# One gather per pick for both expert tables, and weights made for two picks at a time

## The reference

```python
q = (xb @ w_query).reshape(tb, PEER_HEADS, 2, PEER_KEY_DIM // 2)
s = jnp.einsum('thpd,pnd->thpn', q, sub_keys)
top_s, top_i = lax.top_k(s, k)                                    # k = 16, of 2 x 128 keys
cand_s = top_s[:, :, 0, :, None] + top_s[:, :, 1, None, :]
best_s, best_j = lax.top_k(cand_s.reshape(tb, PEER_HEADS, k * k), k)
...
gate = jax.nn.softmax(best_s, axis=-1)
u = expert_u[idx]                                                 # tables of 16384 x 1024
act = jax.nn.gelu(jnp.einsum('thkd,td->thk', u, xb))
w = gate * act
return jnp.einsum('thk,thkd->td', w, expert_v[idx])
```

## Time and profile before

| | |
|---|---|
| median of 3 runs | 1893.31 us (1893.27 to 1904.49) |
| the profiled execution | 1906.0 us, of it the span 1904.2 us |
| busy in the span: PE, DVE, ACT, POOL | 1487.1, 1110.6, 357.7, 1052.6 us |
| moved | 616.74 MB, mean 324 GB/s |

### The profile page before, as it was taken

The page is one execution under the profiler, slowest core; times in us unless marked ns, Lnnn a source line. Parts: engine busy times, 40 slices in busy tenths (PEclk is TensorE's granted clock), DMA queues, the critical chain, the costliest instruction groups (busy, mean ns, idle before and its releaser), DMA issues.

```text
span 1904.2 us, 14545 instructions
## 1 busy us (share of the span) xinstructions
PE 1487.1 (78%) x4063; PEld 675.9 (35%) x4063; DVE 1110.6 (58%) x2719; ACT 357.7 (19%) x910; POOL 1052.6 (55%) x1111
## 2 busy tenths in 40 slices
PE   8999977498887774799988874988888738767776
PEld 3466544145322221344433522433334313222222
DVE  3344255686555555765786656666876556645552
ACT  1033202112221111121221111221211211111110
POOL 1111033666666666556676565766665657656664
PEclk9999997798999987899989997999999979998999
DMA  5112046999998888799999997999999889988897
GB/s 180 63 72 74 15 168 237 418 345 350 370 384 353 352 342 348 294 362 392 417 418 418 370 381 301 396 418 417 418 418 399 319 331 356 384 338 347 346 383 260
DMA packets 184126, 616.74 MB, mean 324 GB/s; under 512 B 19275, under 2 KB 20811, under 8 KB 184054
## 3 DMA queue, kind: packets, MB, share of 16 engines
q0 software_dynamic: 152064, 553.72, 74.5%
q1 hardware_dynamic: 31990, 62.17, 8.7%
HBM read 614.77 MB, written 1.05 MB: 323 GB/s over the span
## 4 chain that ended last, share of the span: by engine, by line
PE 30%; DVE 19%; DMA 15%; issue 14%; POOL 13%; another core or an unknown queue 8%; ACT 0%; DVEq 0%; SPq 0%; POOLq 0%
POOL arena L607 13%; PE bank L892 11%; DMA arena<-peer_u,idx 9%; PE bank L685 8%; DVE arena L1602 8%; DMA arena<-peer_v,idx 5%; PE bank L866 2%; PE bank L787 2%; PE bank L793 2%; DMA wring<-gla_w_in 1%; PE bank L748 1%; PE bank L759 1%; DVE best L1549 1%; PE bank L841 1%
## 5 line engine op out<-in xcount | busy, mean ns | idle before, releaser
L892 PE MATMUL bank<-arena 128*128 128x512 f32 x1920 | 953.7, 636 | 339.6 <-DMA arena<-peer_v,idx 164.5
L1602 DVE CUSTOM_DVE_ANT_0 arena<-arena,bank 128x1024 f32<-128x1024 f32 x528 | 625.3, 1217 | 274.2 <-DMA arena<-peer_u,idx 188.1
L607 POOL DMA_INDIRECT arena<-peer_u,idx x528 | 511.7, 969 | 337.9 <-issue 140.0
L892 PEld LDWEIGHTS bank<-arena 128*128 128x128 f32 x1920 | 359.9, 199 | 892.3 <-issue 454.6
L607 POOL DMA_INDIRECT arena<-peer_v,idx x528 | 511.2, 968 | 281.6 <-issue 149.7
L685 PE MATMUL bank<-wring,hT 128*128 128x512 f32 (+5 forms) x604 | 262.2, 589 | 5.0 <-issue 2.8
L1197 ACT ACTIVATE arena<-con,wgt 128x128 f32<-128x128 f32 x480 | 153.3, 390 | 356.3 <-issue 170.6
L685 PEld LDWEIGHTS bank<-wring,hT 128*128 128x128 f32 (+1 forms) x604 | 108.8, 182 | 151.7 <-issue 145.1
L1186 ACT ACTIVATE gl<-dots 128x16 f32<-128x16 f32 x33 | 7.1, 216 | 401.3 <-issue 228.8
L572 POOL TENSOR_TENSOR small<-small,con 128x1 f32<-128x1 f32 (+2 forms) x12 | 8.1, 677 | 120.3 <-DVEq L1368 71.1
L1611 DVE SCALAR_TENSOR_TENSOR h<-arena,wgt,h 128x1024 f32<-128x1024 f32 x48 | 61.6, 1284 | 20.7 <-DMA arena<-peer_v,idx 20.7
(11 more groups left out here) (157 smaller groups left out, 1011.3 us busy)
## 6 DMA issues: line engine op xcount, KB each, us to landing
wring<-gla_w_in SPq DMA_DIRECT2D x12, 2048.0 KB
arena<-peer_u,idx POOLq DMA_INDIRECT x528
arena<-peer_v,idx POOLq DMA_INDIRECT x528
wring<-gla_w_out SPq DMA_DIRECT2D x4, 2048.0 KB
wring<-peer_w_query SPq DMA_DIRECT2D x4, 2048.0 KB
wring<-attn_w_in SPq DMA_DIRECT2D x2, 2048.0 KB
wring<-attn_w_out SPq DMA_DIRECT2D x2, 2048.0 KB
gws<-peer_w_query SPq DMA_DIRECT2D x2, 2048.0 KB, 10.3
```

What stands on the lines that cost most here:

```text
L607: nc.gpsimd.indirect_dma_start(out=ring[:, slot, :], out_offset=None, in_=table.rearrange("l e d -> (l e) d"), in_offset=bass.IndirectOffs ...
L892: last = nc.tensor.matmul(yacc[:, 512 * i:512 * i + 512], wdiag[:, k, :], vrow[:, v_slot(g, k), 512 * i:512 * i + 512], start=first, stop= ...
L1602: v.tensor_tensor_reduce(out=rows, in0=rows, in1=xnow, scale=1.0, scalar=0.0, op0=ALU.mult, op1=ALU.add, accum_out=dots[:, g % 2, k:k + 1] ...
```

## The change

It lays the two tables side by side on the host, outside the measured time, as `peer_uv` with rows of 8 KB. One gather brings a pick's pair of rows into one ring of eight pairs, and a pair's slot is free when its v rows have been mixed or added. GpSimd issues one gather where it issued two. Gelu, weight and diagonal are made for pairs of picks: `gelus(i, j)` when both dots are done, `weigh` after the dot that follows them, `diagonals(i, j)` after that. TensorE mixes tile i in tile i, so `FIRST` moves each mixer pass a tile earlier, `add_experts` comes at pick 3 of the next tile, and 33 rounds stand where 34 stood. The selection is cut in three, after dots 1, 4 and 7, in every tile. Tile 0 has all of tile 1's selection after its dot 7. VectorE no longer takes six picks of the last tile. ScalarE's pieces have places by pairs (-1 is ahead of the first). In the windowed attention the products of block 2 with block 0, which its mask makes zero, are dropped, and a transpose of block 0 is narrower.

```diff
-U_RING, V_RING = 8, 9
+RING = 8
...
-LEAD = 4
-ADD_BEHIND = LEAD + 2
+GROUP = 2
+GROUPS = TOPK // GROUP
...
-        FIRST = {1: 10, 2: 18}
+        FIRST = {1: 9, 2: 17}
...
-        TENSOR_AT = ((7, 11, 12, 15), (1, 2, 5, 9), (2, 3, 8, 9, 12), (0, 4, 6, 10, 12), (2, 6, 10), (0, 3, 12), (0, 5, 9, 12))
+        TENSOR_AT = ((7, 11, 12, 15), (1, 2, 5, 9), (2, 3, 8, 9, 12), (0, 4, 6, 10, 12), (2, 4, 10), (0, 3, 12), (0, 5, 9, 12))
         VECTOR_AT = ((5, 10), (8, 12), (4, 14), (12,), (3, 6, 10), (10, 12), ())
-        SCALAR_AT = ((3,), (0, 2, 3), (0, 2), (0, 1, 2), (0, 1, 2), (0,), (0, 1), (0,))
+        SCALAR_AT = ((5,), (-1, 1, 4, 5), (-1, 3, 6), (2, 3), (-1, 0, 3), (-1,), (-1, 1, 4), (-1,))
...
-            if g == TILES - 1:
-                return LAST_SHARE
-            return SHARE if mixer_turn(g + 1)[0] and mixer_turn(g + 1)[1] < len(TENSOR_AT) else ()
+            return SHARE if mixer_turn(g)[0] and mixer_turn(g)[1] < len(TENSOR_AT) else ()
...
-            def gather(kind, g, k):
-                layer = GATHERED[g][0]
+            def gather(g, k):
                 n = TOPK * g + k
-                if kind == 0:
-                    at_least(pool, u_used, n - U_RING + 1)
-                elif n >= V_RING:
-                    wait_second_used(pool, (n - V_RING) // TOPK, (n - V_RING) % TOPK)
-                table, ring, landed = ((io["peer_u"], urow, u_in), (io["peer_v"], vrow, v_in))[kind]
-                slot = n % (U_RING, V_RING)[kind]
+                if n >= RING:
+                    wait_second_used(pool, (n - RING) // TOPK, (n - RING) % TOPK)
                 nc.gpsimd.indirect_dma_start(
-                    out=ring[:, slot, :], out_offset=None, in_=table.rearrange("l e d -> (l e) d"),
-                    in_offset=bass.IndirectOffsetOnAxis(ap=idx[:, g % 4, k:k + 1], axis=0)).then_inc(landed[slot], 16)
-            def chosen(g):
-                pool.wait_ge(idx_ready, g + 1)
+                    out=uvrow[:, n % RING, :], out_offset=None, in_=io["peer_uv"].rearrange("l e d -> (l e) d"),
+                    in_offset=bass.IndirectOffsetOnAxis(ap=idx[:, g % 4, k:k + 1], axis=0)).then_inc(uv_in[n % RING], 16)
...
-            chosen(0)
-            for k in range(U_RING):
-                gather(0, 0, k)
-            small_root(1)
-            for k in range(U_RING, TOPK):
-                gather(0, 0, k)
-            for k in range(8):
-                gather(1, 0, k)
-            chosen(1)
-            for k in range(TOPK):
-                gather(0, 1, k)
-                if k < 8:
-                    gather(1, 0, k + 8)
-            for i in range(2, TILES + 1):
+            for i in range(TILES):
                 full, turn = mixer_turn(i)
-                if i < TILES:
-                    chosen(i)
+                pool.wait_ge(idx_ready, i + 1)
                 for k in range(TOPK):
-                    if i < TILES:
-                        gather(0, i, k)
-                    if k >= LEAD:
-                        gather(1, i - 1, k - LEAD)
-                    elif i > 2:
-                        gather(1, i - 2, TOPK - LEAD + k)
-                    if k == 13 and i in (2, EARLY, 26):
+                    gather(i, k)
+                    if k == 5 and i == 0:
+                        small_root(1)
+                    if k == 10 and i in (2, EARLY, 26):
                         small_root({2: 2, EARLY: 0, 26: 1}[i])
-                    if k == 13 and full and turn == 0 or k == 15 and full and turn == 5:
+                    if k == 10 and full and turn == 0 or k == 14 and full and turn == 5:
                         small_root(full)
                     if k == 11 and full and turn == 4:
                         root(gms[:, 0:4], gms[:, 4:8], 4)
-            for k in range(TOPK - LEAD, TOPK):
-                gather(1, TILES - 1, k)
             small_root(2)
...
+            def head_values(hh, windowed):
...
                 for b in range(NB):
-                    for kb in range(b + 1):
+                    keys = range(1, 3) if windowed and b == 2 else range(b + 1)
+                    for kb in keys:
                         n = live_parts(kb)
                         at = KEY_BLOCKS.index((b, kb)) if kb else b
                         last = nc.tensor.matmul(bk(6, b * HD, b * HD + HD), probT[0:n, int(kb == 0), at * P:at * P + P],
-                                                v_all[0:n, kb, hh, :], start=(kb == 0), stop=(kb == b))
+                                                v_all[0:n, kb, hh, :], start=(kb == keys[0]), stop=(kb == b))
...
-                    wait_landed(pe, 1, g, k)
+                    wait_landed(pe, g, k)
                     pe.wait_ge(diag_ready, MIXED[g] + mine.index(k) + 1)
                     for i in range(2):
                         last = nc.tensor.matmul(yacc[:, 512 * i:512 * i + 512], wdiag[:, k, :],
-                                                vrow[:, v_slot(g, k), 512 * i:512 * i + 512], start=first, stop=last_one)
+                                                rows_of(g, k, 1)[:, 512 * i:512 * i + 512], start=first, stop=last_one)
...
-            for i in range(1, TILES + 1):
+            for i in range(TILES):
...
-                    mix(i - 1, (k,))
+                    mix(i, (k,))
...
-                    if k == 3 and i + 2 < TILES and not late:
+                    if k == scores_at and 0 < i and i + 2 < TILES:
                         scores(i + 2)
-                    if k == 4 and full and turn == 6:
-                        scores(i + 1)
-                    if k == 13 and full and turn == 6:
-                        scores(i + 2)
...
-            def gelus(g):
-                act.wait_ge(dots_ready, g + 1)
-                nc.scalar.activation(gl[:, :], dots[:, g % 2, :], ACT.Gelu_apprx_tanh).then_inc(gelu_ready, 1)
-            def diagonals(g, half):
-                act.wait_ge(wgt_ready, g + 1)
+            def gelus(g, j):
+                c = slice(GROUP * j, GROUP * j + GROUP)
+                act.wait_ge(u_used, TOPK * g + GROUP * j + GROUP)
+                nc.scalar.activation(gl[:, c], dots[:, g % 2, c], ACT.Gelu_apprx_tanh).then_inc(gelu_ready, 1)
+            def diagonals(g, j):
+                act.wait_ge(wgt_ready, GROUPS * g + j + 1)
                 for k in by_tensor(g):
-                    if k // (TOPK // 2) != half:
+                    if k // GROUP != j:
...
+                for j in range(GROUPS):
+                    gelus(i, j)
+                    if j == GROUPS - 1 and i + 1 < TILES and (i == 0 or GATHERED[i + 1][2] == 0):
+                        take_rows(i + 1)
+                    diagonals(i, j)
+                    if j in at:
+                        next(pieces)
+                    if j == 2 and i + 1 < TILES:
+                        gate_exps(i + 1)
+                    if j in (2, 4, 7) and i == 3:
+                        take_queries(0, 2, (2, 4, 7).index(j))
+                    if j == 6 and i == 2:
+                        take_T("tr_ffn0", 2)
+                        take_gains(2)
...
-            def choose_experts(g):
-                layer = GATHERED[g][0]
+            def choose_sums(g):
                 best16(cand[:, :], cand_rest[:, :], best, best_j)
...
                 dve.sem_inc(best_ready, 1)
+            def choose_experts(g):
...
-                wait_landed(dve, 0, g, k)
-                rows = urow[:, u_slot(g, k), :]
+                wait_landed(dve, g, k)
+                rows = rows_of(g, k, 0)
                 v.tensor_tensor_reduce(out=rows, in0=rows, in1=xnow, scale=1.0, scalar=0.0,
                                        op0=ALU.mult, op1=ALU.add, accum_out=dots[:, g % 2, k:k + 1]).then_inc(u_used, 1)
-                if g and k - ADD_BEHIND in by_vector(g - 1):
-                    add_second(g - 1, k - ADD_BEHIND)
...
-                wait_landed(dve, 1, g, k)
                 at_least(dve, v_added, ADDED[g] + by_vector(g).index(k))
-                v.scalar_tensor_tensor(out=h[:, b, :], in0=vrow[:, v_slot(g, k), :], scalar=wgt[:, g % 2, k:k + 1], in1=h[:, b, :],
+                v.scalar_tensor_tensor(out=h[:, b, :], in0=rows_of(g, k, 1), scalar=wgt[:, g % 2, k:k + 1], in1=h[:, b, :],
                                        op0=ALU.mult, op1=ALU.add).then_inc(v_added, 1)
-            def dotted(g):
-                dve.wait_ge(gate_exp, g + 1)
+            def weigh(g, j):
                 zs = z[:, g % 2, :]
-                steps.did(v.reciprocal(zs[:, 2:3], zs[:, 1:2]))
-                dve.wait_ge(u_used, TOPK * (g + 1))
-                dve.sem_inc(dots_ready, 1)
-            def weigh(g):
-                zs = z[:, g % 2, :]
-                if g >= 2:
-                    dve.wait_ge(diag_ready, MIXED[g - 1])
-                    at_least(dve, v_added, ADDED[g - 1])
-                steps.settle()
-                dve.wait_ge(gelu_ready, g + 1)
```

(50 more changed lines are left out.)

71 lines of the change are left out of this document (20 added, 51 removed).

## The result

| | kernel before | changed kernel |
|---|---|---|
| median, us (runs) | 1893.64 (4) | 1789.53 (4) |
| lowest to highest | 1893.27 to 1904.49 | 1780.09 to 1794.79 |
| profiled span | 1904.2 | 1789.1 |

A forecast was written before the change was run, and what follows sets the result against it. It took the DMA engines at 418 GB/s (2.51 us per pick) as the bound, with VectorE's gaps slowing clean tiles. Stage terms summed to 1805.5 us against the profiled 1904.2, scaled to 1795 us; range 1735 to 1890.

The forecast's parts named there:

- The main term: Clean tiles, which load no weights: a single gather removes nearly all of VectorE's gaps, 48 to 40.5 us each.
- the gaps: VectorE's idle time in the selection, 15.5 us in one clean tile; rival that they stay, chance 0.12, about 1885 us.
- A sign of being wrong that came: Clean tiles: the prediction is wrong if GpSimd waits more than 5 us at a time.
- its two others: Signs of being wrong: mixer passes below 370 GB/s, or VectorE's gaps of 4.71 us still there.
- The rival of eight pairs too few: Ring: tolerance passed three times a tile, +5 us in each of 26 tiles, median 1924 us; chance 0.13.
- the slot's turn of 14.8 us: Ring: time a pair holds its slot; eight pairs tolerate interruptions of 5.3 us in clean tiles, 8.9 in mixer tiles.
- Start: First tile: pick 4 of tile 1 done at 343 us instead of 331, 12 us lost to GpSimd's wait for slot 0.
- Second pass: Second mixer pass: seven mixer tiles at 50 us each, 350 us, the same value as the first pass.
- Gathers: GpSimd: one 1 MB gather costs between 0.95 and 1.9 us, taken as 0.95; 144 or 272 packets a pair.
- the rival "better": Gathers and mixer tiles: 8 KB rows move faster or mixer tiles reach 47.5 us, median 1736 us; chance 0.10.
- The rule on queues: Weight loads: DMA engines switch queues only between packets, so 8 KB packets could delay weights, TensorE standing 7 us each pass.
- the rival of late weights: Mixer passes: TensorE waits twice 7 us and some for lower clock, median 1815 us; chance 0.03.

The follow-up runs named there:

- experiment 1: Changed kernel with each pair brought by two 512 KB gathers again: 1926.96 us, ratio 1.017 to the kernel before.
- experiment 9: On one chip: the kernel before unchanged (1871.42 us profiled), the changed kernel (1785.64 us), and the changed kernel with two gathers per pair (1925.53 us).
- experiment 8: Changed kernel with start in original order, GpSimd clearing 128x800 and then 128x400 elements of an unread buffer behind each gather: 1804.28 us.
- experiment 10: Changed kernel with a second gather of 64 bytes a row into an unread buffer behind each gather: 1825.30 us.
- the other start: Changed kernel with tile 1's choice spread over the first eight products and two query groups moved after picks 3 and 9 of tile 0: 1788.42 us.
- experiment 3: Changed kernel with GpSimd clearing an unread 128x800 buffer behind each gather: 1808.46 us, ratio 0.954 to the kernel before.
- experiment 2: Kernel before with v gathers bringing 2 KB a row instead of 4: 1882.18 us, ratio 1.008 to the kernel before.
- experiment 6: Changed kernel with the other start, eight pairs: 1788.42 us, ratio 1.030 to the kernel before.
- experiment 7: Changed kernel with nine pairs and the other start together: 1738.23 us, ratio 1.002 to the kernel before.

## Why the prediction was right, and where it wasn't

*Stage by stage.* The terms of the sum against the changed kernel's trace (1789.1 us, of a run of 1790.87):

| stage | predicted us | measured us |
|---|---|---|
| start to tile 1 | 343 | 333.8 |
| tiles 1 to 5 | 231 | 229.9 |
| clean tiles 6 to 8 | 121.5 | 123.0 |
| seven mixer tiles | 350 | 349.8 |
| tile 16 | 41 | 46.2 |
| second pass | 350 | 340.2 |
| tiles 24, 25 | 82 | 82.4 |
| tiles 26 to 30 | 203 | 199.4 |
| end | 84 | 84.4 |
| together | 1805.5 | 1789.1 |

The sum was 16 us too high. It was then scaled by 0.994, since the profiled run of before was a long one, to 1795. The profiled run of the changed kernel was an ordinary one, so that 1795 lies within 6 us of the median is in part luck.

*The main term, clean tiles from 48 to 40.5.* The number is right: 39.9 to 41.0, and the sign it named is there: no idle time ahead of the second MAX8 (L1498), DMA share 1.01. That the gaps go with the single gather was a pattern read from 33 choices. Experiments 1 and 9 bear it out in part, on chips of the first kind: two gathers bring back waits behind the unknown releaser, though hardly in VectorE's choice. The mechanism was seen too narrowly. "Taken alone this is worth nothing while the DMA engines set 2.51" doesn't hold on this kind of chip: with hardly a gap in the choice, two gathers still make a clean tile 46.8 us, and in the second profile of the kernel before GpSimd waits only 2.7 us for VectorE in five clean tiles and yet they take 45.3 each. What the prediction says beside it, "GpSimd is exactly as slow as the DMA engines and never gets ahead", fits better: at 2.50 us a pick GpSimd can't make up for a wait, whatever it is for (table of experiment 9). By itself this pace is a small term, at most 16 us in experiment 8 and 37 in experiment 10, both on the second kind, where GpSimd has few waits on top.

*A sign of being wrong that came.* The prediction called itself wrong if GpSimd waits more than 5 us at a time in clean tiles. It does, seven times in nine clean tiles and 7.81 us at the longest, and costs nothing there: the DMA share stays at 1.01. The sign was set too sharply; its two others (mixer passes below 370 GB/s, gaps of 4.71 us) stayed away, at 389 and 391 GB/s.

*What wasn't seen: the gain belongs to a kind of chip.* The working took the gaps for a property of the kernel. That the comparison fell on a chip of the first kind is luck: on the second kind the time would have lain in the range, but the forecast "faster" would have been wrong. On two of the chips the kernel before takes 1735 us, 157 less, while forms of the changed kernel take what they take on the first kind: 1788.4 with the other start on the second kind, 1785.6 and 1789.5 for the changed one on the first. The changed kernel itself wasn't run on the second kind; from the form with the other start, whose tile 1 comes 5 us sooner, the change makes it some 3% slower there. No profile of the kernel before exists from such a chip, so that its stalls are absent there is inferred from its time and from the profiles of the others. What makes the stalls, and why on some chips, stays open. A full queue (the changed kernel has one, without stalls) and a GpSimd busy half of the time (experiment 3) are ruled out as sufficient, and a full queue isn't needed either (experiment 2). An unbroken row of gathers on a chip of the first kind, with rows of 8 KB, wasn't tested.

*The ring.* The rival of eight pairs too few was set at 3.3 us per tile; it didn't decide, but it is real. With the other start, nine pairs are 50 us faster than eight (1738.2 and 1788.4 on one chip); of that, 1.9 and 2.7 us are saved in each mixer tile of the two passes, 2.4 in each of tiles 1 to 5, and nothing in clean tiles 26 to 30 (traces of experiments 6 and 7). The prediction had this the other way round, with a tolerance of 5.3 us in clean tiles and 8.9 in mixer tiles: it counted the slot's turn of 14.8 us as the same in both. In the first mixer pass GpSimd waits 5 to 9.2 us on TensorE 23 times in seven tiles, against 7 times in nine clean tiles. That ScalarE's and TensorE's other pieces lengthen the turn there is the likely reason, not a measured one. With nine pairs and the other start the loss to the kernel before is all but gone on the second kind (1738.2 and 1734.7).

*Start.* Predicted 343, measured 333.8, the mis-sized term. The prediction took the scores at 305.2 us from the earlier trace rows; they now end at 286.60. The first gather is at 255.78 instead of 259.2, 3.4 us earlier (2.6 on the other chip, 253.45 and 256.00), where 1 was taken for the attention edit from a range of 0 to 5. The rest is TensorE's: its queries run from 268.84 on with hardly a pause, where before they ran from 274.05 with eight pauses of 0.4 to 2.2 us between 283 and 296. First mix at 291.18, not 305, and pick 8 at 300.91, not 313. The silence of 27.01 us on GpSimd is the one that was named ("about 30").

*Tile 16* took 46.2 us, not 41: it follows the mixer pass and was counted as clean, but it stands near 46 with eight pairs and at 47.1 with nine (six: 51.4). On what it waits wasn't looked into. *Second pass*: 340.2 against 350, since one value was used for both though the earlier trace rows had the second at 49.0 against 50.8. The two misses cancel in part.

*End.* 84.41 us for 84.

*Gathers.* 0.947 us in the median for 1 MB (L590), as taken; 144 packets, the lower of the two counts. *8 KB rows move faster*: 427 GB/s against 418, 2%, which was part of the rival "better" and is in clean tiles at 39.9 instead of 40.1.

*The rule on queues.* "DMA: Bandwidth & Descriptors", section "Queues, rings and completion order", of the Trainium skill says that an engine switches between queues only between packets. Packets did become 8 KB, and the waits for a weight group on TensorE's two rows (matmuls and weight loads) didn't grow: 0.7 + 1.5 = 2.2 us in all against 4.9. The section's packet, though, is a run of descriptors, typically 9 to 17; whether the profile's packets are these, no run here shows. So the rule isn't tested, but the rival of late weights is out.

## What to carry to other kernels

Costing a change from an unexplained idle time is costing it for one chip: compare the kernel before on a second chip before trusting a gain that comes from a wait the profile can't name. Where an engine that only issues work is as slow as the transfers, compare its issuing with the length of a stage: where the two are close, it can't make up for a wait of any kind, and a change that halves its issuing is worth more than the one gap it was made for. Where two buffers of a pair are merged, count the slot's whole turn in the stage with the most other work between its steps, and try one more slot before judging the merge. A gather with rows twice as long costs GpSimd no more to issue (0.95 us) and moves slightly faster (427 GB/s for 418), so merging gathers is good as long as depth doesn't pay for it.

## What the runs showed of the hardware

- A gather of 128 rows costs GpSimd 0.95 us and 0.30 to the next for rows of 8 KB (L590), 4 KB (L607) and 64 bytes (experiment 10), in the median.
- Rows of 8 KB go as one packet each, and the engines reach 427 GB/s with them, 418 with 4 KB.
- The kernel before takes 1735 us on two chips (20 runs, 1732 to 1739) and 1891 to 1894 us in the medians of three comparisons elsewhere. The changed kernel took 1789.5 and 1785.6 us in two of those, and its form with the other start 1788.4 us on a chip of the second kind.
- With two gathers a pick GpSimd's issuing takes 2.5 us a pick, 199.5 of 233.4 us in five clean tiles; 33.7 more are waits.
- With GpSimd clearing memory (experiment 8), VectorE's cast of 128x32 values took 0.32 us in the median and up to 1.56, where the changed kernel has 0.18 and at most 0.44. Timeline of VectorE there, one of the long ones:

```profile
1598.88 1.34 DVE L1533 CAST top_f<-top_i 128x32 f32<-128x32 uint32 x1
```
